# Stick-breaking attention: the mask added to the scores in PSUM, the second scores made early, state-space steps split at their scans

## The reference

```
def stick_breaking_attention(q, k, v):          # 4 heads of 64
    def block(qi, t):
        earlier = key_pos[None, :] < t[:, None]
        z = einsum('bqhd,bshd->bhqs', qi, k) * scale
        log_fail = where(earlier, log_sigmoid(-z), 0.0)
        log_between = cumsum(log_fail, axis=3, reverse=True) - log_fail
        w = where(earlier, exp(log_sigmoid(z) + log_between), 0.0)
        return einsum('bhqs,bshd->bqhd', w, v)
```

## Time and profile before

| | |
|---|---|
| median of 3 runs | 3841.4 us (3839.28 to 3844.2) |
| the profiled execution: time | 3847.1 us |
| its span, first to last instruction | 3845.4 us |
| TensorE busy | 3446.5 us (90%) |
| VectorE busy | 2873.0 us (75%) |
| ScalarE busy | 1480.1 us (38%) |
| GpSimd busy | 1020.2 us (27%) |
| mean granted TensorE clock | 0.954 |

### The profile page before, as it was taken

The page is one execution under the profiler, slowest core; times in us unless marked ns, Lnnn a source line. Parts: engine busy times, 40 slices in busy tenths (PEclk is TensorE's granted clock), DMA queues, the critical chain, the costliest instruction groups (busy, mean ns, idle before and its releaser), DMA issues.

```text
span 3845.4 us, 58583 instructions
## 1 busy us (share of the span) xinstructions
PE 3446.5 (90%) x20122; PEld 1992.1 (52%) x20122; DVE 2873.0 (75%) x5232; ACT 1480.1 (38%) x1978; POOL 1020.2 (27%) x742
## 2 busy tenths in 40 slices
PE   7899988979798889999888999889787979999997
PEld 3444644546464556666444446345454546566663
DVE  5765435898979768888847654368989896788887
ACT  4324423335353533333333244223343535333333
POOL 0510100231413134444324100002323141344442
PEclk9999998989999999999998899999998999999998
DMA  5001312586869699999540013126778786999995
GB/s 172 29 1 50 127 55 77 204 285 238 319 208 317 217 375 370 374 387 371 212 143 12 1 61 116 55 88 234 259 270 285 239 322 212 377 368 379 384 369 189
DMA packets 386162, 840.91 MB, mean 219 GB/s; under 512 B 32608, under 2 KB 231264, under 8 KB 385248
## 3 DMA queue, kind: packets, MB, share of 16 engines
q1 hardware_dynamic: 311712, 565.38, 42.0%
q0 software_dynamic: 73728, 268.47, 19.0%
q10 hardware_dynamic: 576, 5.37, 0.4%
HBM read 732.14 MB, written 106.95 MB: 218 GB/s over the span
## 4 chain that ended last, share of the span: by engine, by line
PE 31%; DVE 9%; DMA 3%; issue 3%; ACT 2%; SPq 2%; DVEq 0%; POOL 0%; ACTq 0%
PE ps L1635 4%; PE ps L1637 4%; PE ps L1636 4%; PE ps L116 3%; PE ps L117 3%; PE ps L118 3%; DMA wf<-experts 2%; SPq L82 2%; DVE wl L95 1%; DVE xT L1794 1%; DMA xT<-urows,small 1%; PE ps L152 1%; ACT wh L89 1%; ACT xh L181 0%; DVE small L1759 0%
## 5 line engine op out<-in xcount | busy, mean ns | idle before, releaser
L116 PE MATMUL ps<-xh,wh 128*128 128x384 f16 (+1 forms) x2880 | 1007.1, 350 | 215.2 <-DVE wl L95 62.9
L95 DVE SCALAR_TENSOR_TENSOR wl<-wf,wh 128x1024 f16<-128x1024 f32 x656 | 804.1, 1227 | 443.9 <-ACT wh L89 421.7
L89 ACT ACTIVATE wh<-wf 128x1024 f16<-128x1024 f32 x656 | 690.7, 1053 | 1025.2 <-PE ps L1637 582.3
L117 PE MATMUL ps<-xl,wh 128*128 128x384 f16 (+1 forms) x2880 | 1005.4, 349 | 0.0
L118 PE MATMUL ps<-xh,wl 128*128 128x384 f16 (+1 forms) x2880 | 1003.8, 349 | 0.0
L1734 POOL DMA_INDIRECT xT<-urows,small x256 | 363.4, 1419 | 1170.6 <-DVE xT L1794 888.6
L1635 PE MATMUL ps<-work,wh 128*128 128x384 f16 x2048 | 667.7, 326 | 6.0 <-DVE work L1919 4.3
L1637 PE MATMUL ps<-work,wl 128*128 128x384 f16 x2048 | 667.6, 326 | 0.0
L1636 PE MATMUL ps<-work,wh 128*128 128x384 f16 x2048 | 667.6, 326 | 0.0
L1742 POOL DMA_INDIRECT work<-experts,small x256 | 453.1, 1770 | 579.9 <-DVE work L1928 553.6
L116 PEld LDWEIGHTS ps<-xh,wh 128*128 128x128 f16 x2880 | 287.7, 100 | 478.0 <-ACT work L1677 104.5
(11 more groups left out here) (347 smaller groups left out, 4146.2 us busy)
## 6 DMA issues: line engine op xcount, KB each, us to landing
wf<-experts SPq DMA_DIRECT2D x512, 512.0 KB
wf<-proj SPq DMA_DIRECT2D x144, 512.0 KB
gates<-work SPq DMA_DIRECT2D x48, 1024.0 KB
work<-hid SPq DMA_DIRECT2D x256, 192.0 KB
work<-gates SPq DMA_DIRECT2D x256, 192.0 KB
hid<-work SPq DMA_DIRECT2D x192, 192.0 KB
hid<-small SPq DMA_DIRECT2D x64, 192.0 KB
xsave<-xT ACTq DMA_DIRECT2D x2, 2048.0 KB, 7.0
```

Source lines behind the costliest of these rows:

```text
L89: m.nc.scalar.activation(m.wh[:, slot, :], m.wf[:, k, :], ACT.Copy, scale=WS).then_inc(m.high_done, 1)
L95: m.nc.vector.scalar_tensor_tensor(m.wl[:, slot, :], m.wf[:, k, :], WS, m.wh[:, slot, :], ALU.mult, ALU.subtract).then_inc(m.split_done, 1)
L116: m.nc.tensor.matmul(out, wh[:, k, :], xh[:, k, 0:n], start=(k == order[0]), stop=False)
L117: m.nc.tensor.matmul(out, wh[:, k, :], xl[:, k, 0:n], start=False, stop=False)
```

## The change

The 0/1 tile `before` is replaced by `barred`, which is 0 where the key is earlier and -1e30 elsewhere. `sb_scores` adds it, by a matmul with the identity, to the first 128 columns of each block: L544 of the changed kernel, four more matmuls on 128 rows behind the four scores. Barred pairs then have |z| so large that softplus and weight come out as 0, and the multiplies L1089 and L1099 are gone. The second scores are made by the same function, so they too get the four mask matmuls, and they no longer wait for softplus: they wait for the two readers of the first scores (`act_step`, and the new semaphore `sb_rl` of the relu). The sums are a function of their own, `sb_sums`.

```
         def sb_scores(h, last_of_group):
             rows = slice(64 * (h % 2), 64 * (h % 2) + 64)
             for s in range(NT):
                 o, n = sb_cols(s)
-                last = MM(m.zb[:, o:o + n], ksb[rows, h // 2, s * P:(s + 1) * P],
-                          qsb[rows, h // 2, s * P:], start=True, stop=True)
+                MM(m.zb[:, o:o + n], ksb[rows, h // 2, s * P:(s + 1) * P], qsb[rows, h // 2, s * P:],
+                   start=(o % SEQ == 0), stop=False)
+                last = MM(m.zb[:, o:o + P], m.ident[:, :], m.barred[:, :], start=False,
+                          stop=last_of_group and s != 1)
...
+        ssm_in(0)
+        for h in range(BH):
+            st = h * PER_HEAD
+            if h:
+                ssm_out(st - 2)
+            pe.wait_ge(m.sb_rl, h + 1)
+            pe.wait_ge(m.act_step, 3 * h + 1)
+            sb_scores(h, False)
+            ssm_in(st + 1)
+            if h:
+                sb_values(h - 1)
+            sb_sums(h)
             if h == 0:
                 turned_queries(1)
-            ssm_in(st + 1)
+            else:
+                ssm_out(st - 1)
+            ssm_in(st + 2)
             if h + 1 < BH:
                 pe.wait_ge(m.sb_w, h + 1)
-                sb_scores(h + 1).then_inc(m.sb_z, 1)
-                if h:
-                    ssm_out(st - 1)
-                sb_values(h)
-                ssm_out(st)
-                ssm_in(st + 2)
+                sb_scores(h + 1, True).then_inc(m.sb_z, 1)
...
         for h in range(BH):
             dve.wait_ge(m.act_step, 3 * h + 1)
-            step(TS(rl[:, :], m.zb[:, 0:SB_W], SB_SCALE, 0.0, ALU.mult, ALU.max))
-            dve.wait_ge(m.act_step, 3 * (h + 1))
-            step(TT(sp_[:, :], sp_[:, :], rl[:, :], ALU.add))
-            for s in range(NT):
-                o, _n = sb_cols(s)
-                last = TT(sp_[:, o:o + P], sp_[:, o:o + P], m.before[:, :], ALU.mult)
-            last.then_inc(m.sb_sp, 1)
+            if h:
+                dve.wait_ge(m.sb_sp, h)
+            TS(rl[:, :], m.zb[:, 0:SB_W], SB_SCALE, 0.0, ALU.mult, ALU.max).then_inc(m.sb_rl, 1)
             if h == 0:
                 turn_queries(0)
-            ssm(h * PER_HEAD)
+            else:
+                ssm_first(h * PER_HEAD)
+            dve.wait_ge(m.act_step, 3 * (h + 1))
+            dve.wait_ge(m.sb_rl, h + 1)
+            TT(sp_[:, :], sp_[:, :], rl[:, :], ALU.add).then_inc(m.sb_sp, 1)
+            if h == 0:
+                ssm_first(h * PER_HEAD)
+            ssm_second(h * PER_HEAD)
             if h == 0:
                 turn_queries(1)
-            dve.wait_ge(m.sb_w, h + 1)
-            for s in range(NT):
-                o, _n = sb_cols(s)
-                last = TT(wt[:, o:o + P], wt[:, o:o + P], m.before[:, :], ALU.mult)
-            last.then_inc(m.sb_wm, 1)
-            ssm(h * PER_HEAD + 1)
+            ssm_first(h * PER_HEAD + 1)
+            ssm_second(h * PER_HEAD + 1)
```

More of the change, by code:

```diff
@@ L324, in _ @@
             nc.gpsimd.memset(m.full[:, :], -1.0 / SB_SCALE)
+            nc.gpsimd.memset(m.barred[:, :], 0.0)
             nc.gpsimd.memset(m.rows[:, 0:1], 0.0)
@@ L338, in _ @@
                     (m.tri, m.full, ALU.is_ge, 0, -1, 1, 0.0),
-                    (m.before, m.ones, ALU.is_gt, 0, 1, -1, 0.0)):
+                    (m.barred, m.barred, ALU.is_gt, 0, 1, -1, NEG)):
                 nc.gpsimd.affine_select(out=out[:, :], in_=src[:, :], pattern=[[step_, P]], compare_op=op,
@@ L535, in tensor, with sb_scores @@
         pe.sem_inc(m.tile_used, RING)
-        def sb_scores(h):
+        def sb_scores(h, last_of_group):
             rows = slice(64 * (h % 2), 64 * (h % 2) + 64)
@@ L561, in tensor @@
         pe.wait_ge(m.evac, T_VSB)
-        sb_scores(0).then_inc(m.sb_z, 1)
+        sb_scores(0, True).then_inc(m.sb_z, 1)
         pe.wait_ge(m.weights, 16 * N_SMALL)
@@ L635, in sb_values @@
             rows = slice(64 * (h % 2), 64 * (h % 2) + 64)
-            pe.wait_ge(m.sb_wm, h + 1)
+            pe.wait_ge(m.sb_w, h + 1)
             if h == 2:
@@ L643, in sb_values, with sb_sums @@
             last.then_inc(m.sb_o, 1)
-        ssm_in(0)
-        for h in range(BH):
-            st = h * PER_HEAD
+        def sb_sums(h):
             pe.wait_ge(m.sb_sp, h + 1)
-            rows = slice(64 * (h % 2), 64 * (h % 2) + 64)
             for s in range(NT):
                 o, n = sb_cols(s)
-                MM(m.zb[:, o:o + n], ksb[rows, h // 2, s * P:(s + 1) * P], qsb[rows, h // 2, s * P:],
-                   start=True, stop=False)
                 last = MM(m.zb[:, o:o + n], m.tri[:, :], sp_[:, o:o + n], start=False, stop=(s == NT - 1))
@@ L657, in tensor @@
                     last = MM(m.zb[:, o + n - n2:o + n], m.full[:, :], sp_[:, o2:o2 + n2],
-                              start=False, stop=(s2 == NT - 1))
+                              start=False, stop=(s2 == NT - 1 and s != 1))
             last.then_inc(m.sb_t, 1)
+        ssm_in(0)
[10 more added lines that the diff above has]
+            sb_sums(h)
             if h == 0:
                 turned_queries(1)
-            ssm_in(st + 1)
+            else:
+                ssm_out(st - 1)
+            ssm_in(st + 2)
             if h + 1 < BH:
                 pe.wait_ge(m.sb_w, h + 1)
-                sb_scores(h + 1).then_inc(m.sb_z, 1)
-                if h:
-                    ssm_out(st - 1)
-                sb_values(h)
-                ssm_out(st)
-                ssm_in(st + 2)
+                sb_scores(h + 1, True).then_inc(m.sb_z, 1)
         def mla_s(i):
@@ L702, in mla_o @@
             last.then_inc(m.mla_av, 1)
-        ssm_out(ST_SB - PER_HEAD - 1)
         sb_values(BH - 1)
@@ L709, in tensor @@
         mla_s(1)
-        ssm_in(ST_SB)
         ssm_out(ST_SB - 1)
@@ L1072, in ssm_skip, with ssm_first @@
                 B[2 + j % 2].rearrange("p (i k) -> p i k", i=2), ALU.mult, ALU.add).then_inc(m.ssm_y, 1)
-        def ssm(st):
+        def ssm_first(st):
             ssm_turn(st)
@@ L1078, in ssm, with ssm_second @@
             step(ssm_scan(st, 1))
+        def ssm_second(st):
             ssm_back(st)
@@ L1975 @@
 lat_done up rot rot_done ssm_exp ssm_args ssm_trig table ssm_bu ssm_mul ssm_prod ssm_read
-ssm_y sb_z sb_sp sb_t sb_w sb_wm sb_o sb_y mla_sc mla_nm mla_e mla_p mla_tr mla_pt mla_av mla_y
+ssm_y sb_z sb_sp sb_t sb_w sb_rl sb_o sb_y mla_sc mla_nm mla_e mla_p mla_tr mla_pt mla_av mla_y
 gelu_done glu_in glu_mm glu_sig glu_done grp_sq grp_sum y_norm yh_done yl_done
@@ L2003, in program @@
          m.ssm_exp, m.ssm_args, m.ssm_trig, m.table, m.ssm_bu, m.ssm_mul, m.ssm_prod, m.ssm_read,
-         m.ssm_y, m.sb_z, m.sb_sp, m.sb_t, m.sb_w, m.sb_wm, m.sb_o, m.sb_y, m.mla_sc, m.mla_nm, m.mla_e,
+         m.ssm_y, m.sb_z, m.sb_sp, m.sb_t, m.sb_w, m.sb_rl, m.sb_o, m.sb_y, m.mla_sc, m.mla_nm, m.mla_e,
          m.mla_p, m.mla_tr, m.mla_pt, m.mla_av, m.mla_y, m.gelu_done, m.glu_in, m.glu_mm, m.glu_sig,
@@ L2039, in program @@
         m.rs = sb("rs", [P, 2, SEQ])
-        m.ident, m.ones, m.full, m.tri, m.before = (
-            sb(n, [P, P]) for n in ("ident", "ones", "full", "tri", "before"))
+        m.ident, m.ones, m.full, m.tri, m.barred = (
+            sb(n, [P, P]) for n in ("ident", "ones", "full", "tri", "barred"))
         m.eps, m.eps_ln, m.freq = sb("eps", [P, 1]), sb("eps_ln", [P, 1]), sb("freq_sb", [P, 2])
```

## The result

The changed kernel takes 3888.59 us (median of four runs, 3883.11 to 3898.43) against 3842.8 us for the kernel before on the same chip: a ratio of 1.012, with a 95% interval of 1.0094 to 1.0146. It is 45.8 us slower, where 23 were forecast. That is inside the range of 3834 to 3892 us, and it is the time of rival 3.

What follows compares the result with a forecast made beforehand. TensorE's queue and its lowered clock were taken to bound the stage. Masks +31.6, new wait +2.7, old waits -11.3, present clock loss -28 and later loss C = 28 gave +23 us: 3864.4 us, range 3834 to 3892.

Steps and rivals of the forecast that it cites:

- rival 3: Low clock starting at an ssm_in lasts until values or sums; clock loss 50 to 70 us, 3886 to 3906 us; chance 0.12.
- What bounds the kernel: In the stick-breaking stretches of both layers: TensorE's own queue nearly bounds, plus 28 us of work lost to low clock.
- Masks on TensorE: Four 128x128 mask products in each score group, alternating with 64-row scores: 3.95 us a head, +31.6 us over both layers.
- The waits for VectorE: TensorE's waits for masked softplus at the second scores, five places over both layers, vanish: -11.3 us.
- The new wait: Second scores wait for absolute value and relu to read the bank: 0.45 us in three heads a layer, +2.7 us.
- The sums: Triangular and full sums after the second scores, taken from head 3 of the first layer as 5.11 us.
- The clock, C = 28 us: Work lost to TensorE's low clock in the two stretches, assumed to stay 28 us; bounds 0 and 40, longer stretches 70.
- I take these as equal: Kept narrow matmuls and sums moved further apart, against a 128-row mask product after each score; clock loss left at 28 us.
- the first low stretch of each layer: Low-clock stretches near 119.5 and 2027.3 us, ahead of the first head's sums: 3.4 and 1.7 us, left alone by the change.
- the upper bound: Slow end of the forecast range, 3892 us, set to leave out the upper half of the lasting-low-clock case.
- Rival 1: A gapless TensorE queue keeps the clock up in the two stretches: clock loss 0 to 12, 3836 to 3849 us; chance 0.20.

Runs made afterwards that it cites:

- the fastest kernel: Kernel before the change, masks on VectorE and old order kept, with keys zero-padded to 128 rows, tiles cleared and keys turned early: 3814.61 us, ratio 0.992.

## Why the prediction was right in its mechanism and wrong in its largest term

**What bounds the kernel** was right: TensorE's queue and its clock.

**Masks on TensorE, +31.6 us:** right, 31.3. 4.60 us measured for a group, 4.62 forecast, and the pair price of unlike rows was then shown directly (4.60 with alternation, 3.44 without, 3.25 with like rows).

**The waits for VectorE, -11.3 us:** right, all gone, and by the dropped multiplies alone.

**The new wait, +2.7 us:** right in size where it shows (0.45 us), too many in number: it was seen twice, 0.9 us. At the low clock ssm_out takes 4.54 us instead of 2.41 (167.48 to 172.02) and covers the readers.

**The sums** were taken as 5.11 us a head and cost 4.53. That is a gain of 4.6 us which the prediction left out. The likely reason is the price of unlike rows again: no 64-row scores stand between the sums any more.

**The clock, C = 28 us:** this is the step that failed, in the sentence "I take these as equal and let the loss stay what it was". The mechanism was right as far as it went, narrow matmuls in a busy queue: with 128-row scores the clock goes from 0.78 to 0.96, and without any alternation from 0.95 and 0.83 to 0.96 and 0.95. It left out that the alternation lowers the clock too. The size was wrong: the loss is 65 us against 32, +33.5 where 0 was put. The prediction named the reason against its own value, 22 us of other work between two groups of sums instead of 15, and set a mask product against it. The masks turned out not to balance it but to add to it: with the order of before they too lower the clock, 0.89 and 0.86 to 0.84. In the prediction's own way of counting, half of the low time less the first low stretch of each layer, C is 73 - 7 = 66, and the sum -5 + 66 - 4.6 - 1.8 = 55 us. It is 48.5, mostly since the work at the low level takes 1.8 to 1.9 times as long, not twice. So the median landed inside the range only because the upper bound took in half of rival 3; the forecast itself was half of what was measured.

**Rival 1** (a gapless queue keeps the clock up) is excluded: 23.70 of 23.70 us busy, at 0.50. The Trainium skill, TensorE: Matmul & The Clock Gate, section Part 1: The HAM clock gate, describes a monitor of how busy TensorE is; if busy means instructions in the queue, the trace does not agree. Idle time does go with a low clock as well: in the fastest kernel the clock falls at waits of 1.20 and 0.90 us behind an ssm_in (184.77 and 208.58 us) and stays up over like steps without a wait. But it needs no idle time: even with padded keys one short low stretch a layer is left that starts in the busy queue (at 148 us in layer 1), behind two ssm_in steps with only one score group between them.

**Rival 3** is what happened, with the place it named: the low clock that starts at an ssm_in lasts until the values or sums.

## What to carry to other kernels

Before moving work onto TensorE or reordering it, list each stretch of matmuls by the rows they use and by where the rows change, and look at the granted clock of the stretches like it: a full queue in which 64-row scores, 32-row and 64-row steps and 128-row masks took turns ran at half clock here for up to 27 us. Padding the contraction to 128 rows with zeros cost a matmul nothing here (2.35 us for four, 64 rows or 128) and brought 30 us on the kernel before, 26 of them in the two stretches, more than all the 11.3 us of waits that the change went after. And when a term of the sum rests on two opposing effects that are "taken as equal", its bounds belong into the forecast: ask first which way the doubt points.

## What the runs showed of the hardware that was not expected

- Four scores take 2.35 us on 64 rows and on 128. Beside 128-row masks they make a group of 4.60 us on 64 rows, 3.25 us on 128.
- At the low level a group of scores and masks takes 1.8 times as long (8.34 us instead of 4.60), four scores without masks 1.9 times (201.92 to 206.48 us of the kernel before, 4.56 us instead of 2.35).
- Rows in use and alternation of unlike rows each lower the clock of a busy queue; with 128 rows throughout the alternation costs neither time nor clock.
- The same instruction order ran one layer at 0.95 and the next at 0.83 (masks in a block).
